# Half of the feed-forward block moved beside the expert gather of a two-block transformer kernel, and every second weighted row of that stretch added on VectorE

## The reference, cut to what matters

```python
def block(args):                      # PEER, first block
    xt, it, gt = args
    act = jax.nn.gelu(jnp.einsum('td,tkd->tk', xt, peer_u[it]), approximate=False)
    return jnp.einsum('tk,tkd->td', gt * act, peer_v[it])
...
x = x + g1 * (mixed @ w_out[l])       # second block, after its mixer
h = rms_norm(x, norm2_g[l]) * (1 + sc2) + sh2
u = causal_depthwise_conv(h @ w_up[l], conv_w[l], conv_b[l])   # 3 taps: t, t-1, t-2
u_gate, u_val = jnp.split(u, 2, axis=-1)
x = x + g2 * ((jax.nn.silu(u_gate) * u_val) @ w_down[l])
```

## Time and profile before

| | us |
|---|---|
| median of 3 runs | 2731.71 (2725.87 to 2734.3) |
| the profiled execution, whole | 2735.58 |
| its span in the profile | 2733.8 |
| PE / DVE / ACT busy in the span | 2214.5 / 1671.2 / 1017.9 |
| POOL busy in the span | 713.1 |
| DMA in the span | 682.67 MB, mean 250 GB/s |

### The profile page before, as it was taken

The page is one execution under the profiler, slowest core; times in us unless marked ns, Lnnn a source line. Parts: engine busy times, 40 slices in busy tenths (PEclk is TensorE's granted clock), DMA queues, the critical chain, the costliest instruction groups (busy, mean ns, idle before and its releaser), DMA issues. The chain is left out here.

```text
span 2733.8 us, 25164 instructions
## 1 busy us (share of the span) xinstructions
PE 2214.5 (81%) x7846; PEld 1352.5 (49%) x7846; DVE 1671.2 (61%) x3405; ACT 1017.9 (37%) x2518; POOL 713.1 (26%) x619
## 2 busy tenths in 40 slices
PE   5999868897888777777868887658776967799988
PEld 5778644476533232322324453223333834588777
DVE  5652456544598898878456776647666533555434
ACT  4213235513244333333334444436433433433322
POOL 1000214001244444443434544435442100100000
PEclk8999869998999999898989999878897959799999
DMA  6773200022299999999999999989997511222122
GB/s 198 227 214 97 66 5 23 19 82 102 115 422 420 421 396 421 404 421 404 418 376 420 421 419 418 406 339 407 421 420 288 144 46 47 94 97 102 61 85 100
DMA packets 142490, 682.67 MB, mean 250 GB/s; under 512 B 19440, under 2 KB 36112, under 8 KB 73888
## 3 DMA queue, kind: packets, MB, share of 16 engines
q0 software_dynamic: 73728, 536.90, 47.6%
q1 hardware_dynamic: 68640, 144.30, 16.2%
HBM read 679.05 MB, written 2.10 MB: 249 GB/s over the span
## 5 line engine op out<-in xcount | busy, mean ns | idle before, releaser
L1791 PE MATMUL peer_Y<-peer_w,peer_diag 128*128 128x512 f32 x1792 | 909.5, 648 | 230.6 <-ACT peer_diag L1777 205.1
L1736 POOL DMA_INDIRECT peer_w<-in_peer_uv,peer_eidx x512 | 603.7, 1179 | 757.0 <-PE peer_Y L1791 477.2
L1745 DVE CUSTOM_DVE_ANT_0 peer_w<-peer_w,peer_xtok 128x1024 f32<-128x1024 f32 x512 | 620.3, 1222 | 208.4 <-DMA peer_w<-in_peer_uv,peer_eidx 204.8
L1791 PEld LDWEIGHTS peer_Y<-peer_w,peer_diag 128*128 128x128 f32 x1792 | 342.9, 204 | 746.1 <-ACT peer_diag L1777 428.4
L1769 ACT ACTIVATE peer_gel<-peer_dots 128x1 f32<-128x1 f32 x512 | 103.8, 203 | 723.6 <-DVE peer_dots L1745 719.3
L1777 ACT ACTIVATE peer_diag<-all_ident,peer_a 128x128 f32<-128x128 f32 x448 | 179.9, 402 | 17.4 <-PE peer_Y L1791 2.9
L1771 ACT ACTIVATE peer_a<-peer_gel,peer_gates 128x1 f32<-128x1 f32 x512 | 150.9, 295 | 16.7
L2278 PE MATMUL ffn_acc<-m2f_hs,ffn_cut 128*128 128x512 f32 x352 | 138.3, 393 | 9.4 <-DVE ffn_cut L2326 9.4
L654 DVE TENSOR_TENSOR p_cut<-m1h_raw,p_cut 128x512 fp32r<-128x512 f32 (+2 forms) x96 | 63.2, 660 | 126.3 <-ACT p_cut L680 126.3
L2279 PE MATMUL ffn_acc<-m2f_hs,ffn_cut 128*128 128x512 f32 x352 | 138.0, 392 | 0.0
L2280 PE MATMUL ffn_acc<-m2f_hs,ffn_cut 128*128 128x512 f32 x352 | 137.9, 392 | 0.0
(11 more groups left out here) (466 smaller groups left out, 3823.1 us busy)
## 6 DMA issues: line engine op xcount, KB each, us to landing
m_gates<-in_w_ada SPq DMA_DIRECT2D x48, 512.0 KB, 4.3
m2f_raw<-in_w_up SPq DMA_DIRECT2D x22, 1024.0 KB, 4.8
m1h_raw<-in_w_in SPq DMA_DIRECT2D x80, 256.0 KB, 3.0
m20h_raw<-in_w_in SPq DMA_DIRECT2D x48, 256.0 KB, 7.1
m22h_raw<-in_w_in SPq DMA_DIRECT2D x48, 256.0 KB, 3.2
m_down_ring<-in_w_down SPq DMA_DIRECT2D x22, 512.0 KB, 3.5
peer_w<-in_peer_uv,peer_eidx POOLq DMA_INDIRECT x512
m_out_ring<-in_w_out SPq DMA_DIRECT2D x16, 512.0 KB, 8.6
```

The lines of the kernel that those rows point to most:

```text
L1736: pool.indirect_dma_start(self.w[:, n % self.RW].rearrange("p c n -> p (c n)"), None, self.uv_dram, bass.IndirectOffsetOnAxis(self.col(sel ...
L1745: dve.tensor_tensor_reduce(u, u, self.xtok[:, n // PICKS, :], 1.0, 0.0, ALU.mult, ALU.add, self.col(self.dots, n)).then_inc(self.dotted, 1)
L1791: ins = pe.matmul(self.Y[:, h, :], self.diag[:, i % self.RD, :], self.w[:, n % self.RW, 1, h * BANK:(h + 1) * BANK], start=(k == 0), stop= ...
```

## The change

The feed-forward part is split into tokens 0 to 255 and tokens 256 to 511. The first half (names f0) runs inside the hosted stretch, after m20o, and carries 72 gather steps: 8 in its norm, 40 in `ffn_up`, 24 in `out_project`. The mixer's five hosted stages keep 10, 60, 36, 40 and 28 of theirs, 174 instead of 246, so the hosted steps stay 246 and `finish_gather` keeps 10. The second half (names f2) runs last, alone. Both halves load all of `w_up` and `w_down`. `ffn_up` is written for any number of tokens: its unit is one column block (128 x 1024 weights, 24 matmuls of 258 columns, the two extra being the last two tokens of the half before, kept in `ends`), hosted with three weight buffers and two cut buffers, alone with four and four; it is unrolled, where before it was a loop on each engine. The hosted `out_project` begins to load `w_down` only when it starts (`ahead=False`), since its ring takes the room of the one before. SHARE is 2: every second step of the second half of the gather goes to DVE.

```diff
@@ norm_transpose
+            side.gpsimd(pool, 0)
@@ out_project
-            for c in range(R, kchunks):
-                sp.wait_ge(lo_made, c - R + 1)
+            for c in range(R if ahead else 0, kchunks):
+                if c >= R:
+                    sp.wait_ge(lo_made, c - R + 1)
                 sp.dma_start(raw[:, c % R, :], w_dram[c * P:(c + 1) * P, :]).then_inc(landed[c % R], 16)
@@ Gather
-    SHARE = 4
+    SHARE = 2
@@ peer_and_front
         second_front(nc, consts, resid, mod, d, kept, HALF, xtok[:, 0:2, :], qT[:].rearrange("p h q -> p (h q)"), pacer)
...
+        second_ffn(nc, consts, resid, mod, d, kept, HALF, lambda c: wide[:, c, :] if c < 2 * PEER_H else narrow[:, c - 2 * PEER_H, :],
+                   xtok[:, 0:2, :], out, pacer)
         finish_gather(nc, gather, pacer.next)
@@ ffn_up
+    UNITS = 2 * NF
+    CUT = 2 if side.BANKS else 4
+    LEFT = 2
...
         @block.tensor
         def _(pe):
...
+            for u in range(UNITS):
+                bank = acc[:, u % 4, 0:LEFT + tokens]
+                hi, lo = cut[:, u % CUT, 0], cut[:, u % CUT, 1]
+                pe.wait_ge(lo_made, u + 1)
+                if u >= 4:
+                    pe.wait_ge(conved, u // 2 - 1)
+                for k in range(KD):
+                    pe.matmul(bank, hi[:, k, :], hs[:, 0, k, :], start=(k == 0), stop=False)
+                    pe.matmul(bank, hi[:, k, :], hs[:, 1, k, :], start=False, stop=False)
+                    ins = pe.matmul(bank, lo[:, k, :], hs[:, 0, k, :], start=False, stop=(k == KD - 1))
                 ins.then_inc(done, 1)
...
+                if u % 4 == 3:
+                    side.tensor(pe, u // 4)
...
         @block.scalar
         def _(act):
...
+            def tail(j):
+                act.wait_ge(done, 2 * j + 2)
+                if j >= 2:
+                    act.wait_ge(out, j - 1)
                 for g in range(2):
...
+                    ins = act.activation(x[:, j % 2, g, :], acc[:, (2 * j + g) % 4, LEFT:LEFT + tokens], ACT.Identity,
...
                 ins.then_inc(biased, 1)
...
+                act.wait_ge(conved, j + 1)
+                act.activation(sl[:, j % 2, :], x[:, j % 2, 0, :], ACT.Silu).then_inc(silued, 1)
+
+            for u in range(UNITS):
+                if u >= RAW:
+                    act.wait_ge(landed[u % RAW], 16 * (u // RAW))
+                if u >= CUT:
+                    act.wait_ge(done, u - CUT + 1)
+                act.activation(cut[:, u % CUT, 0], raw[:, u % RAW], ACT.Copy).then_inc(hi_made, 1)
+                if u % 2 and u >= 3:
+                    tail(u // 2 - 1)
+                if u % 4 == 3:
+                    side.scalar(act, u // 4)
...
         @block.vector
...
+            for u in range(UNITS):
+                dve.wait_ge(hi_made, u + 1)
+                dve.tensor_tensor(cut[:, u % CUT, 1], raw[:, u % RAW], cut[:, u % CUT, 0].bitcast(F32), ALU.subtract).then_inc(lo_made, 1)
+                if u % 2 and u >= 3:
+                    conv(u // 2 - 1)
+                elif u >= 4:
+                    gate(u // 2 - 2)
+                if u % 4 == 3:
+                    side.vector(dve, u // 4)
@@ second_front
-                               keep=space, side=side(14, n))
+                               keep=space, side=side(10, n))
...
-                    beside = side(85, len(jobs) * KD)
+                    beside = side(60, len(jobs) * KD)
...
-            gla(nc, name + "l", consts, qkT, gv, lowT, grT, gla_tables, mixT, kept.state, group, [], side(50, 7 + n))
+            gla(nc, name + "l", consts, qkT, gv, lowT, grT, gla_tables, mixT, kept.state, group, [], side(36, 7 + n))
...
-                  tiles=group, side=side(52, DIL_H * n // 2 + 1))
...
+                  tiles=group, side=side(40, DIL_H * n // 2 + 1))
@@ second_ffn
...
+                           side=side(8, len(group)), col0=2)
...
+                   side(40, NF // 2))
...
+        out_project(nc, name + "o", gT, d["w_down"], NF, resid, out_ring, gate=kept.rows[:, 1, :], out_dram=out, tiles=group,
+                    side=side(24, 2 * NF - 2), ahead=not hosted)
@@ program
...
-                second_ffn(nc, consts, resid, mod, d, kept, out)
+                with Phase(nc, "last") as ph3:
+                    gT = ph3.sb("gT", [P, NF, 2 * P])
+                    second_ffn(nc, consts, resid, mod, d, kept, (2, 3), lambda c: gT[:, c, :], None, out)
```

More of the change, by code:

```diff
@@ L1924, in peer_and_front @@
                 top = TopK(top_ph, tables["iota"], eidx, gates, picked)
[L1925 removed]
+                peer_query(nc, xs, xtok, row["gain"], qT, ring, row, top, tables["keys"], kept.ends)
             Phase.recycle(nc)
@@ L2308, in chunk @@
-                act.activation(sl[:, r, :], u[:, r, 0, :], ACT.Silu).then_inc(silued, 1)
-            split(0, 0, first=True)
-            split(1, 0, first=True)
-            for r in range(R):
-                split(r, 1)
-                chunk(r, 0, first=True)
-            with act.Fori(1, steps - 1) as i:
-                for r in range(R):
-                    split(r, i + 1)
-                    chunk(r, i)
-            for r in range(R):
-                chunk(r, steps - 1)
+                act.wait_ge(conved, j + 1)
@@ L2343, in _, with conv @@
-            split(0, 0)
-            split(1, 0)
-            with dve.Fori(0, steps - 1) as i:
-                for r in range(R):
-                    split(r, i + 1)
-                    chunk(r, i)
-            for r in range(R):
-                chunk(r, steps - 1)
+            link = Link(dve, dve_link)
+            def conv(j):
+                dve.wait_ge(biased, j + 1)
+                for tap, made in ((1, tap1), (0, conved)):
+                    lag = 2 - tap
+                    for g in range(2):
+                        y = x[:, j % 2, g, :]
+                        ins = dve.scalar_tensor_tensor(y, acc[:, (2 * j + g) % 4, LEFT - lag:LEFT - lag + tokens],
+                                                       cw[:, 6 * j + 3 * g + tap:6 * j + 3 * g + tap + 1], y, ALU.mult, ALU.add)
+                    ins.then_inc(made, 1)
+                    dve.wait_ge(made, j + 1)
```

140 lines of the change are left out of this document (55 added, 85 removed).

## The result

The changed kernel takes 2811.79 us (median of 4 runs, 2809.84 to 2817.16) against 2733.01 for the kernel before in the same comparison (2725.87 to 2736.98): a ratio of 1.0294, 95% interval 1.0268 to 1.032, so about 80 us slower. The profiled execution took 2817.16 us, its span is 2815.4.

What follows compares the result with a forecast made beforehand. The prediction took VectorE's chain, its own work plus waits for ScalarE, as mostly the bound. Profiled 2735.6 us + 254 in the hosted stretch - 165 in the tail = 2825, rounded up to 2830, range 2735 to 2905.

Steps and rivals of the forecast that it cites:

- The tail: Norm, up and down stages of the last 256 tokens: 240 us against 405, so 165 us saved.
- VectorE's round: Tail up stage: a pair of column blocks takes 6.3 us through VectorE and its ScalarE waits, against TensorE's 5.8.
- The hosted stretch: Mixer stages 558 us plus hosted feed-forward half 382 come to 940 against 686: 254 us more.
- The check by a sum of waits: m20p before the change: VectorE's 169.7 busy, 70 waiting for ScalarE and 9.3 for DMA make 249 us against 240.
- The up stage: Hosted up stage with 40 gather steps: eleven periods of 19.3 us and 6 at the ends, 218 us.
- The down stage: Hosted down stage with 24 steps: 22 chunks of 5.2 us, 9 for loads, 6 at the end, 130 us.
- The folded rows: Hosted stretch: 61 more rows at 1.28 us each put 79 us more work on VectorE.
- A: DMA is the only bound: the hosted stretch grows by 82 us, time 2653, faster; chance 0.07.
- B: Hosted waits shrink to 150 to 200 us: time 2725 to 2790, faster if the stretch is under 851; chance 0.15.
- C: Hosted half paced by the down stage's slot loop (23 to 73 us more) or TensorE's clock (some 50); chance 0.18.
- D: Matmuls of 258 columns cost as much as 512, 0.229 us: 84 + 103 us more, 3017; chance 0.03.
- E: The hosted half does not run beside the gather: 420 us instead of 382, time 2868; chance 0.02.

Runs made afterwards that it cites:

- e2: The kernel before with every second weighted row on VectorE instead of every fourth: 2732.87 us, ratio 1.0003 to the kernel before.
- e4: The kernel before with no weighted row on VectorE, all on TensorE: 2741.88 us, ratio 1.0039 to the kernel before.
- e9: The kernel before with ScalarE's weight splits ahead of the gather steps in m20p and m20o: 2731.41 us, ratio 1.0001 to the kernel before.
- e7: The changed kernel with ScalarE's next weight split ahead of the gather steps in hosted stages with weight splits: 2770.01 us, ratio 1.0147 to the kernel before.
- e5: The changed kernel with the hosted feed-forward half's weight loads cut to an eighth: 2802.21 us, ratio 1.0266 to the kernel before.
- e6: The changed kernel with gelu in place of silu in the hosted half, so no table change: 2815.83 us, ratio 1.0316 to the kernel before.
- e1: The changed kernel with every fourth weighted row on VectorE instead of every second: 2793.29 us, ratio 1.0223 to the kernel before.

## Why the prediction was right, and where it was not

2830 was forecast and 2811.79 measured, slower, by the mechanism of the forecast: the hosted feed-forward half costs more beside the gather than it saves at the end.

- **The tail**: 240 forecast, 235 measured (15 + 145 + 80 against 14 + 139 + 82). The up stage was forecast at 22 x 6.3 + 6 by VectorE's round. TensorE sets it: it is busy for 132.5 of 139 us, 6.0 a pair, so the step that put VectorE's round ahead of TensorE's 5.8 was wrong, and the numbers lay close enough that it cost little.
- **The hosted stretch**: 940 forecast, 944 measured, as a sum of misses. The mixer's stages took 540 and not 558, the norm 32 (34), the up stage 252 (218), the down stage 120 (130). That 18, 2 and 10 too much and 34 too little come to 4 is luck. VectorE was busy for 674.7 us (695).
- **What bounds the kernel before**: "the bound is mostly the chain on VectorE" was wrong. With more work on VectorE (e2), with less (e4) and with nearly all of its waits for ScalarE gone (e9), m20p took 238 to 241 us at 419 GB/s. I took the row of a wait for the bound. It says which of two came last at one instruction. The check by a sum of waits (249 against 240) tests nothing: an engine's busy time and its waits add up to the stage whatever bounds it, here 169.7 + 61.0 + 9.3 = 240.0. The row that decided was there: a DMA share of 1.02 at 419 GB/s, the same rate as in m20o at 421.
- **Why the sign was still right**: the changed kernel leaves that bound. With 72 steps fewer the mixer's stages gave back 146 us, between the 128 of the forecast and the 180 that DMA alone would have given. In the changed m20p ScalarE is late for 28 splits, and it runs at 390 GB/s; with the splits moved ahead (e7) it is at 420 again and 18 us shorter. In the feed-forward stages DMA has 269 and 302 GB/s to do. There the time goes by VectorE's work and its turns through ScalarE, as the prediction counted, though the next two points show terms with the wrong size.
- **The up stage, 34 us over**: 7 of them belong to the down stage. VectorE's last product of the up stage ends at 2208.06 us, and the line between the stages was drawn at 2215, inside its wait for the first chunk of `w_down`. For the rest the mis-sized term is VectorE's wait for ScalarE, 73.2/11 = 6.65 us in a period where the prediction had 1.4 + 1.65 + 0.45 = 3.5. Averaged over the ten periods after the first, the three waits are 1.15, 2.19 and 3.18. So the one behind the gather steps was priced well, and the one that was put at 0.45, for TensorE and the cut buffers, is seven times that, since the load of eight of the ten fourth blocks comes late: the prediction gave the loads of the up stage no term. The split ahead of the gather steps takes 18 of the 73 us away (e7). Of the 33.8 us of waits for the load 12.7 went when it brought an eighth, for 6 us of the stage (e5): its delay is mostly not its bytes. The tables are worth nothing (e6).
- **The down stage**: VectorE's first split starts at 2216.17 us after a wait of 8.1 for the first load (9 forecast), 22 chunks take 5.16 each (5.2), and 5 follow at the end (6). Nearly all of the first load lies before the line at 2215, so the stage came out at 120 where it is some 127; the forecast of 130 was near in each term.
- **The folded rows**: the prediction charged all of them as VectorE's work, 79 us. They cost 19 in the changed kernel (e1) and nothing in the kernel before (e2).
- **The signs**: the hosted stretch ended at 2335 us (2340 forecast), m20p ran at 390 GB/s (370), the feed-forward stages under 320, POOL waited 488.9 us for folded rows to free its buffers, and VectorE never waited for data there. The waits behind the gather steps were 1.98 and 0.31 us (2.0 and 0.8).

The rivals. A, DMA as the only bound, was right of m20p in the kernel before and wrong of the changed kernel, where VectorE's and ScalarE's turns did not fit beside the transfers. B, shrinking waits, fell: VectorE stood still for 269 us of the hosted stretch, not for 150 to 200. The earlier splits bring it to 219 (894 - 675, e7); with every fourth row on VectorE the stretch is 875 us, and the prediction's line between faster and slower was 851. C is the up stage's excess in kind, though not in its place: a ring of loads held the up stage (33.8 us), while the down stage's slot loop cost nothing and became the next wait once the splits moved (53.0 us). C's other half, TensorE's clock, was not what filled the up stage: it was 0.89 there, TensorE was busy for 188 of 252 us, and ScalarE waited 18.1 us for it. D and E fell: 258 columns cost 0.12 us, and gather steps run in every hosted stage.

What stays open: the hosted up stage takes 222 to 224 us in its best form, 83 more than alone, with 40 gather steps in it. Each edit that eased one of load, cut buffers and ScalarE's order gave at most 19 us there. A fourth weight buffer for the hosted up stage, which its late loads suggest, wasn't tried, nor were two of these eased together without taking a buffer from the gather.

## What to carry to other kernels

Before asking which engine is waited for, ask whether a stage moves the same GB/s as every other full stage: where it does, a wait between engines may be slack, and neither more nor less work on them changed the time here (m20p: 238 to 241 us for VectorE busy 144 to 192). Count the bytes with it, since the gather runs up to nine buffers ahead and its fetches move between stages: m20o took 85 us in the changed kernel and 80 with the earlier splits, both at 426 GB/s, with 29 fetches in it and then with 27. And an engine's busy time plus its waits is always the whole stage, so such a sum can't confirm a bound. Work may be moved beside a DMA-bound stage at little cost only as long as it leaves it DMA-bound; a stage in which each chunk of weights goes through ScalarE, VectorE, TensorE and back brings its own round trip, and guest steps in an engine's order stand in the middle of it. Then look first at that order: putting the split that another engine waits for ahead of the guest's steps gave 40 us for no work, more than any change here of how much work each engine has. After that, look at which split in the period the waits stand before: one period read in order of time showed another place as the worst than the sum over all of them.
